# The low halves of the input projection's weights, split on VectorE instead of GpSimd

## The chip, the cores and the metric

The kernel runs on one core of a Trainium2 chip. The metric is the device time of one execution in microseconds (us). The engines are called PE (TensorE), DVE (VectorE), ACT (ScalarE), POOL (GpSimd) and SP (SyncE, which here issues most DMAs). Each works through its own instructions in the order in which the program lists them, and they wait for one another by semaphores.

## The reference

One layer of a decoder, for a prompt of 1024 tokens and 8 sequences of 4 new tokens each (1056 tokens in all), with a model width of 1024:

```python
h = rmsnorm(x, g_mix_norm)
q, k, v, b_gate, c_gate, hc = split(h @ w_in)       # 512 | 128 | 128 | 512 | 512 | 512
q, k = rope(rmsnorm(q, g_q)), rope(rmsnorm(k, g_k)) # 8 query heads, 2 key heads of 64
o_attn = window_attention(q, k, v, sinks)           # window of 128; new tokens use a cache
u = c_gate * hc
o_conv = b_gate * conv3(u)                          # depthwise, causal, width 3
x = x + concat(rmsnorm(o_attn), rmsnorm(o_conv)) @ w_o
x = x + square(relu(rmsnorm(x) @ w_up)) @ w_down    # 1024 -> 4096 -> 1024
x = x + sigmoid(rmsnorm(x) @ w_ple_gate) * (p @ w_ple)
```

All of it is float32.

## The kernel before

Activations are held with features in the partitions and the 1056 tokens in three chunks of 352 columns. Every large product is made from halves: a float32 matrix w is turned into w_hi, a copy rounded to the type that PE multiplies fast, and w_lo = w - w_hi, and the product is the sum of three: w_hi by x_hi, w_hi by x_lo, w_lo by x_hi.

The work is cut into units. A unit is one tile of 128 output features: 8 tiles of weights (128 x 1024 numbers in all), and for each chunk c of tokens 24 products of 128x128 by 128x352 into the PSUM bank acc[c] (`fill`, L1542, products at L1534). The input projection has 18 units: 0 to 5 make q, k and v, and 6 to 17 make the convolution's inputs in four groups of three (c_gate, hc, b_gate; `which` = 0, 1, 2). Then come 8 units of the output projection, 64 of the MLP and 8 of the gate.

The weights have two slots, used in turn. SP loads a unit's weights into w_st (L522) when the low half of the unit two before it, which used the same slot, has been made. ACT makes w_hi at the head of a unit for the next one, when PE is done with the unit before (`split_hi`, L799 to L805). Then the low half is made (`split_lo`, L498 to L501), and PE waits for it at the start of the next unit (L1700). In the input projection POOL makes the low halves (L757 to L758), but for the first two, which DVE makes while the tokens come in (L1170 to L1173); in all later stages DVE makes them.

Each engine runs one loop over g = 3 * unit + chunk. A list made ahead (`plan_inproj`, L67) puts the steps of attention on it, for 9 tiles of tokens t = 0 to 8, the first with the new tokens, starting at g = 18, 22, 25, 28 and so on. The steps of a tile, by their distance from its start, are: B (0, turn q, k, v to token rows), E (1, norm and rotary), S (3, turn back), Q (4, scores, maxima and exponentials), P and R (6 and 7, turn the probabilities, in two halves), V and W (7 and 8, the output's two halves), N and O (9, norm of the output, and turn it). So the head of each unit from 10 on has step W of one tile.

What the prediction speaks of, by line. On DVE: L1226 and L1228 (step E, low halves of q and k), L1235 (step S), L1281 (P and R, low halves of the probabilities), L1297 and L1305 (V and W, add and scale the output), L1347 (unit with `which` 1: u = c_gate * hc, from PSUM), L1365 (`which` 2: two taps of the convolution for each chunk) and L1372 (times b_gate). On ACT: L805 (high half), L888, L895 and L900 (step S), L935 (W, copies what L1297 adds), L943 (W, square of the output). On POOL: L501 (low half), L735 (W, after L943) and L747 (sum of squares of the convolution). On PE: L1549 (transposes), among them those of the probabilities. At the head of a unit DVE's order is: the convolution's instructions of chunk 0 (L1347, or L1365 twice and L1372, or none), then the steps of attention.

Of the kernel before, what the change touches and what calls it, by code (L numbers as in the profile page):

```python
# [139 lines left out]
def hybrid_step(nc, ins, outs):  # L140
# [149 lines left out]
    with ctx:  # L290
# [134 lines left out]
        def chunk(c):  # L425
            return slice(c * CH, (c + 1) * CH)
# [21 lines left out]
        def conv_parts(c):  # L448

            lo, hi = c * CH, min((c + 1) * CH, SEQ)  # L450
            parts = [(slice(0, hi - lo), (lo, hi))]
            if (c + 1) * CH > SEQ:
                parts.append((slice(SEQ - c * CH, CH), None))
            return parts
# [18 lines left out]
        def done_with(eng, *name):  # L473

            bank, _, before = aux_at[name]
            eng.wait_ge(aux_free[bank], before + 1)
# [21 lines left out]
        def split_lo(eng, s, his):  # L498

            eng.wait_ge(whi_ready, his)  # L500
            eng.tensor_tensor(w_lo[:, s, :], w_st[:, s, :], w_hi[:, s, :], ALU.subtract).then_inc(wlo_ready, 1)  # L501
# [141 lines left out]
        def _(pool):  # L643
# [97 lines left out]
            def add_squares(k):  # L741

                c = k % NCH
                pool.wait_ge(squared, k + 1)
                if k:
                    pool.wait_ge(summed, k)
                pool.tensor_tensor(sq_sum[:, chunk(c)], sq_sum[:, chunk(c)], sq_new[:, :], ALU.add).then_inc(summed, 1)  # L747

            def lo_of_attention(c):

                pool.wait_ge(att_hi, c + 1)
                pool.tensor_tensor(act_lo[:, 0:4, chunk(c)], qkv[:, 0:4, chunk(c)], act_hi[:, 0:4, chunk(c)],
                                   ALU.subtract).then_inc(att_lo, 1)

            for g in range(3 * U_OUT):
                u, c = divmod(g, NCH)
                if c == 0 and u >= 1:  # L757
                    split_lo(pool, (u + 1) % 2, u + 2)  # L758
                gated = u >= U_CONV and (u - U_CONV) % 3 == 2
                if gated and u == U_OUT - 1:  # L760
                    add_squares((u - U_CONV) // 3 * NCH + c)
                for step, t in at[g]:
                    consume(step, t)
                if gated and u < U_OUT - 1:
                    add_squares((u - U_CONV) // 3 * NCH + c)
                if u >= U_CONV and c == 0:
                    j, which = divmod(u - U_CONV, 3)
                    if which == 0:

                        done_with(pool, "C", 0, "c")  # L770
                        if j >= 1:
                            pool.wait_ge(conv_step, CONV_STEPS * j)
                            pool.wait_ge(tail_kept, 2 * j)
                        pool.tensor_copy(u_s[:, :, 0:2], state[:, j, :, :]).then_inc(u_state, 1)
                    if which == 2:

                        pool.wait_ge(acc_free[NCH - 1], u)
                        pool.tensor_copy(tail[:, j, 0:2], u_p[:, SEQ:SEQ + 2]).then_inc(tail_kept, 1)
                        pool.tensor_copy(tail[:, j, 2:2 + 2 * DEC_B].rearrange("p (b s) -> p b s", s=2),
                                         u_s[:, :, DEC_T:DEC_T + 2]).then_inc(tail_kept, 1)  # L780
                if g > 3 * U_OUT - NCH:
                    lo_of_attention(c - 1)
# [6 lines left out]
            for k in range(3 * KT):  # L789
                c = k % (2 * NCH) // 2  # L790
# [352 lines left out]
        def _(dve):  # L1143
# [169 lines left out]
            def norm_conv(c):  # L1313

                done_with(dve, "norm", c, 0)
                dve.reciprocal(root_c[:, c % 2, :], root_c[:, c % 2, :]).then_inc(conv_inverted, 1)
                dve.memset(sq_sum[:, chunk(c)], 0.0).then_inc(sums_cleared, 1)
                dve.wait_ge(conv_inverted, c + 1)
                for k in range(CT):
                    e = dve.scalar_tensor_tensor(out=conv[:, k, chunk(c)], in0=conv[:, k, chunk(c)],  # L1320
                                                 scalar=vec[:, V_CONV + k:V_CONV + k + 1], in1=root_c[:, c % 2, :],
                                                 op0=ALU.mult, op1=ALU.mult)
                e.then_inc(conv_normed, 1)

            def mix_conv(c):

                dve.wait_ge(mix_hi, c + 1)
                dve.tensor_tensor(act_lo[:, 4:8, chunk(c)], conv[:, :, chunk(c)], act_hi[:, 4:8, chunk(c)],
                                  ALU.subtract).then_inc(mix_lo, 1)

            for g in range(3 * U_OUT):
                u, c = divmod(g, NCH)
                if u >= U_CONV:
                    j, which = divmod(u - U_CONV, 3)
                    cw = [vec[:, V_CW + k * CT + j:V_CW + k * CT + j + 1] for k in range(3)]
                    if which == 1:

                        dve.wait_ge(acc_full, g + 1)
                        dve.wait_ge(acc_free[c], u)
                        for cols, tokens in conv_parts(c):  # L1340
                            if tokens is None:
                                dst = u_s[:, :, 2:2 + DEC_T]
                                e = dve.tensor_tensor(dst, acc[c][:, cols].rearrange("p (b s) -> p b s", s=DEC_T), dst,
                                                      ALU.mult)
                            else:
                                dst = u_p[:, 2 + tokens[0]:2 + tokens[1]]
                                e = dve.tensor_tensor(dst, acc[c][:, cols], dst, ALU.mult)  # L1347
                        e.then_inc(acc_free[c], 1)
                    if which == 2:

                        if c == 0:
                            dve.wait_ge(acc_free[NCH - 1], u)
                            dve.wait_ge(const_set, 7)
                            dve.wait_ge(u_state, j + 1)
                        done = CONV_STEPS * j + 2 + 2 * c
                        for cols, tokens in conv_parts(c):
                            for k in range(1, 3):
                                if tokens is None:
                                    dst = conv[:, j, SEQ:NT].rearrange("p (b s) -> p b s", s=DEC_T)
                                    src = u_s[:, :, k:k + DEC_T]  # L1360
                                else:
                                    dst = conv[:, j, tokens[0]:tokens[1]]
                                    src = u_p[:, tokens[0] + k:tokens[1] + k]
                                dve.wait_ge(conv_step, done)
                                dve.scalar_tensor_tensor(out=dst, in0=src, scalar=cw[k], in1=dst, op0=ALU.mult,  # L1365
                                                         op1=ALU.add).then_inc(conv_step, 1)
                                done += 1

                        dve.wait_ge(acc_full, g + 1)
                        dve.wait_ge(conv_step, done)  # L1370
                        dst = conv[:, j, chunk(c)]
                        dve.tensor_tensor(dst, acc[c][:, 0:CH], dst, ALU.mult).then_inc(acc_free[c], 1)  # L1372
                if g == 3 * U_OUT - 2:
                    norm_conv(0)
                if g == 3 * U_OUT - 1:
                    mix_conv(0)
                    norm_conv(1)
                for step, t in at[g]:
                    consume(step, t)
# [142 lines left out]
        def _(pe):  # L1522
            def take_bank(*name):

                bank, _, before = aux_at[name]
                if before:
                    pe.wait_ge(aux_free[bank], before)
                return aux[bank]
# [346 lines left out]
```

## Time and profile before

| | before |
|---|---|
| time, median of 3 runs | 1413.86 us |
| the runs | 1413.86, 1415.95, 1413.68 us |
| span of the profiled execution | 1409.7 us |
| PE, DVE, ACT, POOL busy in it | 1315.8, 716.3, 401.9, 199.2 us |

The profile is of one execution; its own time is given as its span, from the first to the last instruction. The runs' times have some 4 us around that. An engine's busy time is the sum in which it executed an instruction. A chain of waits follows the work back from the last instruction, at each step to what released it. In a timeline each line is an instruction, or several in a row merged; in brackets stands how long its engine had been idle and what released it. The granted clock of PE is given as a share of full speed.

### The profile page before, as it was taken

What the parts mean: (1) busy time and instruction counts of PE and PEld (TensorE: products, weight loads), DVE (VectorE), ACT (ScalarE), POOL (GpSimd) and SP (SyncE); (2) the same over time, 40 slices, a digit from 0 to 9 for tenths busy, and PEclk for the clock granted to TensorE, in tenths of its full rate; (3) what the DMA queues carried; (4) which work ended last, traced back from release to release, by engine and by line L of the source; (5) the groups of instructions that cost most, each with busy time, mean ns of one, the idle gap of its engine ahead of it and who ended that gap; (6) DMA issues with size and microseconds to landing.
All of it is one profiled execution on the core that took longest, in us unless ns stands there. A gap on an engine that the chain in (4) does not pass through costs nothing.

```text
span 1409.7 us, 21751 instructions
## 1 busy us (share of the span) xinstructions
PE 1315.8 (93%) x8348; PEld 1298.5 (92%) x8348; DVE 716.3 (51%) x1271; ACT 401.9 (29%) x801; POOL 199.2 (14%) x216
## 2 busy tenths in 40 slices
PE   3899988997958889999999999999999999999997
PEld 2899877897958889999999999999999999999997
DVE  6302757677575446435445344354453544587342
ACT  5332445455434222102111011121110211254232
POOL 6623434434130000000000000000000000041000
PEclk9999999999989899999999999999999999999999
DMA  5521011001103221321111111111111111111221
GB/s 153 131 60 32 1 48 30 16 16 35 46 17 75 62 65 41 77 52 45 48 47 54 45 45 45 45 45 45 45 45 45 45 50 39 46 45 54 69 68 46
DMA packets 111132, 70.99 MB, mean 50 GB/s; under 512 B 3226, under 2 KB 109622, under 8 KB 111064
## 3 DMA queue, kind: packets, MB, share of 16 engines
q1 hardware_dynamic: 110584, 68.37, 17.7%
q0 software_dynamic: 480, 1.93, 0.5%
q8 instruction: 33, 0.54, 0.2%
q14 instruction: 19, 0.16, 0.0%
q10 hardware_dynamic: 16, 0.00, 0.0%
HBM read 65.69 MB, written 5.54 MB: 51 GB/s over the span
## 4 chain that ended last, share of the span: by engine, by line
PE 77%; DVE 8%; ACT 4%; issue 4%; DMA 3%; POOL 2%; SPq 1%; DVEq 0%; ACTq 0%
PE acc L1534 71%; PE aux L1549 3%; DMA x_col<-in_x_sample 2%; DVE prob L1265 2%; PE aux L1534 1%; POOL act_lo L669 1%; DVE conv L1365 1%; POOL sq_sum L793 1%; DMA w_st<-in_w_in 1%; PE aux L1682 1%; DVE ropea L1218 1%; DVE o_tok L1305 1%; ACT sq_new L1097 1%; DVE pt_lo L1281 1%; ACT w_hi L805 0%
## 5 line engine op out<-in xcount | busy, mean ns | idle before, releaser
L1534 PE MATMUL acc<-xg_hi,w_hi 128*128 128x352 f32 x960 | 312.0, 325 | 0.0
L1534 PE MATMUL acc<-xg_lo,w_hi 128*128 128x352 f32 x960 | 307.8, 321 | 0.0
L1534 PE MATMUL acc<-xg_hi,w_lo 128*128 128x352 f32 x960 | 307.7, 321 | 0.0
L1534 PE MATMUL acc<-a_hi,w_hi 128*128 128x352 f32 x768 | 247.7, 323 | 0.0
L1534 PE MATMUL acc<-a_lo,w_hi 128*128 128x352 f32 x768 | 246.1, 320 | 0.0
L1534 PE MATMUL acc<-a_hi,w_lo 128*128 128x352 f32 x768 | 245.9, 320 | 0.0
L1534 PE MATMUL acc<-act_hi,w_hi 128*128 128x352 f32 x624 | 215.1, 345 | 13.2 <-issue 12.8
L1534 PE MATMUL acc<-act_hi,w_lo 128*128 128x352 f32 x624 | 208.3, 334 | 0.0
L1534 PE MATMUL acc<-act_lo,w_hi 128*128 128x352 f32 x624 | 208.2, 334 | 0.0
L1449 DVE TENSOR_TENSOR xt<-acc,xt 128x352 f32<-128x352 f32 x192 | 100.3, 522 | 179.1 <-PE acc L1534 178.1
L805 ACT ACTIVATE w_hi<-w_st 128x1024 fp32r<-128x1024 f32 x98 | 102.9, 1050 | 280.0 <-PE acc L1534 273.8
L1534 PEld LDWEIGHTS acc<-xg_lo,w_hi 128*128 128x128 f32 x960 | 180.5, 188 | 0.2
L1534 PEld LDWEIGHTS acc<-xg_hi,w_hi 128*128 128x128 f32 x960 | 180.1, 188 | 0.3 <-issue 0.2
L1534 PEld LDWEIGHTS acc<-xg_hi,w_lo 128*128 128x128 f32 x960 | 180.0, 188 | 0.0
L1534 PEld LDWEIGHTS acc<-a_lo,w_hi 128*128 128x128 f32 x768 | 144.3, 188 | 0.0
L1534 PEld LDWEIGHTS acc<-a_hi,w_hi 128*128 128x128 f32 x768 | 144.1, 188 | 0.0
L1534 PEld LDWEIGHTS acc<-a_hi,w_lo 128*128 128x128 f32 x768 | 143.9, 187 | 0.0
L793 POOL TENSOR_TENSOR sq_sum<-sq_sum,sq_new 128x352 f32<-128x352 f32 x24 | 23.2, 966 | 837.8 <-ACT sq_new L1097 837.8
L1534 PEld LDWEIGHTS acc<-act_hi,w_hi 128*128 128x128 f32 x624 | 124.8, 200 | 14.2 <-issue 13.2
L1068 ACT ACTIVATE a_hi<-relu 128x352 fp32r<-128x352 f32 x96 | 47.9, 499 | 292.6 <-DVE relu L1432 292.6
L1432 DVE SCALAR_TENSOR_TENSOR relu<-acc,rstd 128x352 f32<-128x352 f32 x96 | 50.3, 524 | 154.5 <-PE acc L1534 154.5
L1534 PEld LDWEIGHTS acc<-act_lo,w_hi 128*128 128x128 f32 x624 | 124.7, 200 | 0.0
(199 smaller groups left out, 1598.6 us busy)
## 6 DMA issues: line engine op xcount, KB each, us to landing
w_st<-in_w_up SPq DMA_DIRECT2D x32, 512.0 KB, 4.1
w_st<-in_w_down SPq DMA_DIRECT2D x32, 512.0 KB, 3.4
w_st<-in_w_in SPq DMA_DIRECT2D x18, 512.0 KB, 3.9
w_st<-in_w_o SPq DMA_DIRECT2D x8, 512.0 KB, 4.6
w_st<-in_w_ple_gate SPq DMA_DIRECT2D x8, 512.0 KB, 4.3
x_nat<-in_x_prompt SPq DMA_DIRECT2D x11, 352.0 KB
x_col<-in_x_prompt SPq DMA_DIRECT2D x8, 484.0 KB
out<-y_col SPq DMA_DIRECT2D x8, 484.0 KB
```

Of the source, the lines that this page charges most:

```text
L669: pool.tensor_tensor(act_lo[:, 4 * h:4 * h + 4, cols], h_tmp[:, h, :, :], act_hi[:, 4 * h:4 * h + 4, cols], ALU.subtract).then_inc(h_lo, 1)
L793: pool.tensor_tensor(sq_sum[:, chunk(c)], sq_sum[:, chunk(c)], sq_new[:, :], ALU.add)\
L805: act.activation(w_hi[:, s, :], w_st[:, s, :], ACT.Copy).then_inc(whi_ready, 1)
L1068: act.activation(a_hi[:, m, chunk(c)], relu[:, f % 2, :], ACT.Square).then_inc(a_hi_ready, 1)
L1097: act.activation(sq_new[:, :], xt[:, 2 * m + n2, chunk(c)], ACT.Square).then_inc(squared, 1)
L1218: dve.tensor_tensor(heads(ropea, m), qn, cos[:, None, :].broadcast_to([m, NQ + NKV, HD]), ALU.mult).then_inc(cos_ready, 1)
L1265: e = dve.tensor_tensor_reduce(prob[:, h * 2 * P:(h + 1) * 2 * P] .rearrange("p (s k) -> p s k", s=2), bank[:, cols].rearrange("p (s k) -> ...
L1281: frees(dve.tensor_tensor(pt_lo[0:rows_, cols], bank[0:rows_, 0:width], pt_hi[0:rows_, cols], ALU.subtract), step, t, i)
L1432: dve.scalar_tensor_tensor(out=relu[:, f % 2, :], in0=acc[c][:, 0:CH], scalar=0.0, in1=rstd[:, chunk(c)], op0=ALU.max, op1=ALU.mult)\
L1449: dve.tensor_tensor(xt[:, n, chunk(c)], acc[f % 3][:, 0:CH], xt[:, n, chunk(c)], ALU.add)\
L1534: ins_ = pe.matmul(out, w[a][cols], x[b][tile_], start=(k == 0 and p == 0), stop=(k == len(terms) - 1 and p == 2))
L1549: ins_ = pe.transpose(out[dst], src, ident[0:src.shape[0], 0:src.shape[0]])
```

## The change

`split_lo` for the units of the input projection is called on DVE at the head of each unit from 1 on, before everything else that DVE does there, and no longer on POOL. What it waits for (`whi_ready`), computes and signals (`wlo_ready`) is the same; the DVE loop and the POOL loop run over the same g.

```diff
--- before
+++ after
@@ POOL @@
             for g in range(3 * U_OUT):
                 u, c = divmod(g, NCH)
-                if c == 0 and u >= 1:
-                    split_lo(pool, (u + 1) % 2, u + 2)
                 gated = u >= U_CONV and (u - U_CONV) % 3 == 2
@@ DVE @@
             for g in range(3 * U_OUT):
                 u, c = divmod(g, NCH)
+                if c == 0 and u >= 1:
+                    split_lo(dve, (u + 1) % 2, u + 2)
                 if u >= U_CONV:
```

## Rows read from the trace of the kernel before

**Rows 1.** The page: span, busy time by engine, chain by engine.
```profile
span 1409.7 us, 21751 instructions
...
PE 1315.8 (93%) x8348; PEld 1298.5 (92%) x8348; DVE 716.3 (51%) x1271; ACT 401.9 (29%) x801; POOL 199.2 (14%) x216
...
PE 77%; DVE 8%; ACT 4%; issue 4%; DMA 3%; POOL 2%; SPq 1%; DVEq 0%; ACTq 0%
```
**Rows 2.** Busy time by stretch: its length, each engine, PE's granted clock, DMA share, GB/s.
```profile
41.20:131.00 89.80, 89.32 (x565) 88.38 (x564) 14.52 (x24) 29.04 (x57) 35.69 (x39) 1.00 0.25 68
131.00:404.00 273.00, 235.07 (x1576) 226.74 (x1574) 184.50 (x394) 132.01 (x346) 105.92 (x113) 0.94 0.10 27
...
270.90:274.30 3.40, 3.40 (x15) 3.40 (x13) 3.16 (x5) 1.36 (x4) 1.96 (x2) 0.50 0.02 5
218.40:222.50 4.10, 4.10 (x29) 4.06 (x28) 3.44 (x5) 1.31 (x4) 2.58 (x3) 1.00 0.00 0
```
**Rows 3.** Waits, 131 to 404 us: us in total, times, longest.
```profile
ACT aux L943 <- DVE o_tok L1305: 22.2, 8, 4.4
PE aux L1549 <- ACT qt L895: 21.6, 7, 6.3
```
**Rows 4.** Chain of waits, 228 to 246 us: start, us, what.
```profile
237.13 2.59 DVE conv L1365
```
**Rows 5.** Instructions of line 501: shortest, median and longest in ns.
```profile
L501 DVE TENSOR_TENSOR w_lo<-w_st,w_hi x81: 1216/1226/2836, 15.0 to 1372.0; 128x1024 fp32r<-128x1024 f32 x81
L501 POOL TENSOR_TENSOR w_lo<-w_st,w_hi x17: 2346/2398/2772, 63.4 to 380.8; 128x1024 fp32r<-128x1024 f32 x17
```
**Rows 6.** Timeline at the head of unit 14: start, us, instruction.
```profile
314.91 0.42 DVE L1228 TENSOR_TENSOR st_k<-ropea,st_k 128x256 fp32r<-128x256 f32 x1
...
315.24 3.19 DVE L1365 SCALAR_TENSOR_TENSOR conv<-u_p,vec,conv 128x352 f32<-128x352 f32 x2
315.30 2.76 POOL L501 TENSOR_TENSOR w_lo<-w_st,w_hi 128x1024 fp32r<-128x1024 f32 x1 [2.80 <-ACT w_hi L805]
...
318.54 0.53 DVE L1372 TENSOR_TENSOR conv<-acc,conv 128x352 f32<-128x352 f32 x1
...
319.43 0.43 DVE L1305 TENSOR_TENSOR o_tok<-o_tok,stats 128x256 f32<-128x256 f32 x1
319.77 0.58 DVE L1365 SCALAR_TENSOR_TENSOR conv<-u_p,vec,conv 128x352 f32<-128x352 f32 x1
319.89 0.60 ACT L943 ACTIVATE aux<-o_tok 128x512 f32<-128x512 f32 x1 [4.41 <-DVE o_tok L1305]
```
**Rows 7.** Timeline at the head of unit 13.
```profile
289.79 0.42 DVE L1228 TENSOR_TENSOR st_k<-ropea,st_k 128x256 fp32r<-128x256 f32 x1
...
290.12 0.52 DVE L1347 TENSOR_TENSOR u_p<-acc,u_p 128x352 f32<-128x352 f32 x1
290.17 2.38 POOL L501 TENSOR_TENSOR w_lo<-w_st,w_hi 128x1024 fp32r<-128x1024 f32 x1 [2.80 <-ACT w_hi L805]
...
291.00 1.83 DVE L1305 TENSOR_TENSOR o_tok<-o_tok,stats 128x256 f32<-128x256 f32 x1
...
292.87 0.60 ACT L943 ACTIVATE aux<-o_tok 128x512 f32<-128x512 f32 x1 [2.50 <-DVE o_tok L1305]
```
**Rows 8.** Timeline at the head of unit 12.
```profile
263.45 1.18 DVE L1228 TENSOR_TENSOR st_k<-ropea,st_k 128x256 fp32r<-128x256 f32 x1
...
264.87 0.42 DVE L1297 TENSOR_TENSOR o_tok<-aux,cross 128x256 f32<-128x256 f32 x1 [0.24 <-ACT cross L935]
265.33 1.82 DVE L1305 TENSOR_TENSOR o_tok<-o_tok,stats 128x256 f32<-128x256 f32 x1
...
267.18 0.60 ACT L943 ACTIVATE aux<-o_tok 128x512 f32<-128x512 f32 x1 [2.41 <-DVE o_tok L1305]
```
**Rows 9.** Chain of waits: two blocks of 24 products, units 10 and 12.
```profile
218.68 3.86 PE acc L1534 x24
...
271.43 5.21 PE acc L1534 x24
```

## The prediction, before the change was run

> **What bounds the kernel now.** I read the page first. TensorE (PE) is busy for 93% of the span and holds 77% of the chain that ended last; POOL, the engine that the work leaves, is busy for 14% and holds 2%, DVE, which gets it, 51% and 8% [rows 1]. On the page alone the change would be worth nothing, or would cost a little on the busier engine. So the second view was the table by stretches, to see whether the projection is one regime or two. It is two. From 41.2 to 131 us (units 0 to 6) PE is busy for 89.32 of 89.80 us and DVE for 14.52: there it does not matter who splits the weights. From 131 to 404 us (units 7 to 17, beside attention) PE is busy for 235.07 of 273.00 us, so 38 us of it are waits, although no engine is full: DVE 184.50, ACT 132.01, POOL 105.92 [rows 2]. Work passed from engine to engine one link at a time looks like this.
>
> The waits of that stretch name the link: ACT's square L943 waited 22.2 us in 8 waits for DVE's L1305, and PE's transposes L1549 waited 21.6 us in 7 waits for ACT's L895, which stands behind L943 in ACT's order [rows 3]. The chain of waits runs through the same place: a DVE instruction, L1365, with 2.59 us at 237.13 [rows 4]. In most other places it takes 0.58. To see why, one goes to the timeline at the head of a unit, where the moved instruction is.
>
> **Three kinds of head.** Unit u splits the weights of unit u+1 at its head: ACT the high half (L805), then POOL the low half (L501), 2.35 to 2.77 us there. The same instruction on DVE takes 1.22 in the middle, 2.84 at most [rows 5].
>
> In unit 14 POOL runs L501 from 315.30 to 318.06. DVE's pair of L1365 began at 315.24 and took 3.19 us, ending at 318.43, 0.37 after POOL was done; the next L1365 takes 0.58 with POOL idle. So the second of the pair stood still until POOL had finished: 3.19 less 2 x 0.58 and a gap of 0.04 is 1.99 us lost. L1372, L1297 and L1305 follow in DVE's order, and L943 starts 0.03 us after L1305 ends [rows 6]. Units 8, 11, 14 and 17 are of this kind, four heads.
>
> In unit 13 L1347 and L1297 stand there instead and are not stretched, but L1305 takes 1.83 us, against 0.43 in unit 14 with POOL idle, and ends 0.28 after POOL's split: 1.40 lost [rows 6, 7]. Units 10, 13 and 16 are of this kind.
>
> In unit 12 nothing of the convolution stands before L1297, and L1305 takes 1.82: 1.39 lost [rows 8]. Units 12 and 15 are of this kind.
>
> Unit 9 is neither: its tile's L1305 has run before the head, and DVE is idle there. I give it 0, as I do the first seven heads, which lie before or outside the serial stretch.
>
> **What the change removes, adds and moves.** It removes 17 instructions of about 2.4 us from POOL. Nobody waits for POOL's queue at the heads: L735, the next in it, waits for L943 anyway. What counts is that the stalls of DVE beside them go: 1.99, 1.40 and 1.39 us by kind.
>
> It adds 17 instructions on DVE. Their duration I take as the middle of the 81 that DVE has already, 1.22 us [rows 5]; the ends are 1.216 and 2.836. The long one needs POOL reading beside it, and POOL's only neighbour left at a head is the sum of squares L747, which in unit 12 already ends before DVE is free; hence the middle. On DVE consecutive instructions start about 0.08 us before the recorded end of the one before (289.79 plus 0.42 against 290.12 [rows 7]), so one more costs 1.22 - 0.04 to 0.08, some 1.18.
>
> It also adds a wait in DVE's queue: for the high half, by ACT. Queued behind it are L1365 or L1347, L1297 and L1305, and for them ACT and PE. This wait is nearly free: POOL's split starts at 315.30 released by ACT, when DVE's L1228 has just ended (315.33), and in unit 13 at 290.17 against 290.21 [rows 6, 7]. The reason is structural: ACT's high half directly follows the copies for which DVE's L1226 and L1228 wait. In unit 16, the last but one, there is no such copy any more; L1347, which there ran while DVE waited, goes behind the split, and I book that head like the others of its kind.
>
> By kind, with the split put in at the moment when DVE is free and the high half there:
> - units 8, 11, 14, 17: +1.18 - 1.99 = -0.8 each, -3.2 together. In unit 14: split 315.3 to 316.5, the pair to 317.6, L1372, L1297 and L1305 as long as now, L943 at 319.1 instead of 319.89.
> - units 10, 13, 16: +1.18 - 1.40 = -0.2 each, -0.6 together.
> - units 12, 15: L1228 ends at 264.63 and L1297 starts at 264.87, so 0.24 of the split lies in an idle gap, and the overlap hides some more: L1297 moves from 264.87 to 265.69, +0.82, and L1305 is shorter by 1.39: -0.57 each, -1.1 together.
>
> The sum is -4.9 us. What is late next: L943 has behind it on ACT L888, L895, L900 and the rest without a gap, and PE's waits for them, 21.6 us in 7, are 3.1 us each [rows 3], more than any gain. So PE does not become the bound and each gain is handed on whole, through the rest of the projection and to the end, since what follows starts from the end of this chain. In unit 17 the next product of PE may catch a part of the 0.8; a tenth or two. SP's queue gains: its load of the slot waits for the low half, which comes 1.5 us sooner in unit 14 (316.5 for 318.06), but no part of the chain above waits for a load.
>
> **The sum against a time.** The profiled execution has a span of 1409.7 us [rows 1]; the runs have a median of 1413.86, so 4.2 us lie around the span, and I take them as unchanged. 1409.7 - 4.9 = 1404.8 of span, 1408.9 of time, 0.35% less.
>
> **What else moves: TensorE's clock.** From 270.9 to 274.3 us the granted clock was 0.50, the 1.2 GHz level; from 218.4 to 222.5 it was 1.00, which is 2.4 GHz [rows 2]. The block of 24 products in the first took 5.21 us on the chain, in the second 3.86 [rows 9]. A wait that is shorter by 0.2 to 0.8 us can save such a stretch, and work that lies 5 us earlier can meet one elsewhere. One more or less is 1.4 us. I book nothing for it, and two either way in the range: 2.8 us.
>
> **Rivals.**
> *The trade is even.* The port time only changes its owner: 1.4 us of stall against 1.2 of split, as in unit 13, at all nine heads. Then it is 9 x 0.2 = 1.8 us, 1412.1. For it speaks unit 13; against it units 12 and 14, where the stall is longer or the split part hidden. The clock taking back three stretches (4.2 us) ends at the same place. Chance 0.15. The Trainium skill, page "Perfetto Trace Analysis", section "Optimizing Scalar/DVE Operations", warns of this: GpSimd and VectorE share a port to SBUF, so that moving work between the two might not help.
> *Shorter waits keep the clock up.* Three of the slow blocks become fast: 3 x 1.4 = 4.2 on top, 1404.7. For it: PE's waits at the heads, after which such a stretch stands in unit 12, all get shorter. Against: no row shows how short is short enough. Chance 0.13.
> *Slower: the stall stays.* DVE's stretched instructions wait for something else at the head than POOL's split (ACT's L805 reading the same tile, or another of POOL's that comes up into the free place). Then each of nine heads pays the split and gets nothing back: 7 x 1.18 + 2 x 0.82 = +9.9, 1423.8. It decides from about 0.55 us of stall left per head (4.9 over 9). Against it: at all three kinds the stretched instruction ends 0.3 to 0.4 us after POOL's, and the same forms are short at the same place without it. Chance 0.08. Splits of 2.84 us on DVE would end near there too (9 x 1.6 more).
> *It does not do what it says*: PE could wait for low halves that come later now. They come sooner (316.5 against 318.06), and they are needed a whole unit later. I give it nothing apart.
>
> **How the numbers follow.** Forecast 0.64, even trade 0.15, faster clock 0.13, stall stays 0.08. What a measurement of this kernel can tell from no change is 0.2%, 2.8 us, so faster is below 1411.0. Faster: 0.62 of the forecast's 0.64, 0.13, and 0.03 of the even trade, 0.78. Slower: 0.08. The same: 0.14. The forecast's own range is 1406.1 to 1411.7 (two slow blocks either way); with most of the faster clock and the even trade it is 1405.2 to 1412.6.
>
> **What would show it.** Right: L501 on DVE at 1.2 us, 17 more; at heads 8, 11, 14 and 17 L1365 at 0.58, at the others L1305 at 0.43; L943's wait for L1305 shorter; the stretch from 131 us to the first output unit shorter by 5 us and the MLP as long as before. Wrong: a stretched L1365 or L1305 at a head with POOL idle, a split of over 2 us, DVE idle at a head waiting for L805, or more stretches of granted clock 0.50 than now.

## The result, and the profile after

| | before | after |
|---|---|---|
| time, median of 5 runs | 1413.86 us (1412.80 to 1416.46) | 1404.06 us (1397.90 to 1407.85) |
| ratio after/before | | 0.9923, 95% interval 0.9898 to 0.9949 |
| span of the profiled execution | 1409.7 us | 1406.0 us |
| mean granted clock in it | 0.980 | 0.976 |

The kernel became faster, as forecast, but by 9.8 us and not by 4.9; 1404.06 lies 1.1 us under the range. The two profiled spans differ by only 3.7 us. Why the profiles show a smaller gain than the runs is the question of this part.

In the profile after, lines between L757 and L1331 carry numbers smaller by two (L941 is L943 of before, L1303 is L1305, L1226 is L1228). First the page: span, busy time, chain by engine, against [rows 1].

```profile
span 1406.0 us, 21751 instructions
...
PE 1317.5 (94%) x8348; PEld 1299.9 (92%) x8348; DVE 719.5 (51%) x1288; ACT 402.5 (29%) x801; POOL 158.3 (11%) x199
...
PE 80%; DVE 6%; ACT 4%; issue 3%; DMA 3%; POOL 3%; SPq 1%; DVEq 0%; ACTq 0%; POOLq 0%
```

DVE got 17 instructions and is busy for only 3.2 us more, although the splits take it 21 us, so its other instructions take some 18 us less. L1365 alone takes 8.1 us less in all (21.8 before, 13.7 after) and the scaling L1305 7.1 (13.9 and 6.8): the stall that has gone. POOL has 40.9 us less. Next the instructions of line 501, against [rows 5], and of the output's scaling on DVE (shortest, median and longest in ns).

```profile
L501 DVE TENSOR_TENSOR w_lo<-w_st,w_hi x98: 1207/1226/2831, 15.1 to 1368.3; 128x1024 fp32r<-128x1024 f32 x98
```
```profile
L1303 DVE TENSOR_TENSOR o_tok<-o_tok,stats x16: 424/426/427, 200.8 to 382.5; 128x256 f32<-128x256 f32 x16
```

No scaling is stretched any more (1.82 and 1.83 us in units 12 and 13 of before, 0.43 at most here). The head of unit 14, against [rows 6]: start, us, instruction.

```profile
310.45 0.42 DVE L1226 TENSOR_TENSOR st_k<-ropea,st_k 128x256 fp32r<-128x256 f32 x1
...
310.79 1.23 DVE L501 TENSOR_TENSOR w_lo<-w_st,w_hi 128x1024 fp32r<-128x1024 f32 x1
311.93 1.20 DVE L1365 SCALAR_TENSOR_TENSOR conv<-u_p,vec,conv 128x352 f32<-128x352 f32 x2
...
313.24 0.53 DVE L1372 TENSOR_TENSOR conv<-acc,conv 128x352 f32<-128x352 f32 x1
...
314.59 0.60 ACT L941 ACTIVATE aux<-o_tok 128x512 f32<-128x512 f32 x1 [3.56 <-DVE o_tok L1303]
```

From the end of L1226 (310.87) to the start of L941 it is 3.72 us; before, from 315.33 to 319.89, 4.56: -0.84. The split begins 0.08 us before L1226 has ended on the record, and the pair of L1365 takes 1.20. The heads of units 13 and 12, against [rows 7, 8]:

```profile
286.82 0.42 DVE L1226 TENSOR_TENSOR st_k<-ropea,st_k 128x256 fp32r<-128x256 f32 x1
...
287.17 1.23 DVE L501 TENSOR_TENSOR w_lo<-w_st,w_hi 128x1024 fp32r<-128x1024 f32 x1
288.31 0.52 DVE L1347 TENSOR_TENSOR u_p<-acc,u_p 128x352 f32<-128x352 f32 x1
...
289.19 0.43 DVE L1303 TENSOR_TENSOR o_tok<-o_tok,stats 128x256 f32<-128x256 f32 x1
...
289.66 0.60 ACT L941 ACTIVATE aux<-o_tok 128x512 f32<-128x512 f32 x1 [2.25 <-DVE o_tok L1303]
```
```profile
260.91 1.07 POOL L747 TENSOR_TENSOR sq_sum<-sq_sum,sq_new 128x352 f32<-128x352 f32 x1 [2.23 <-ACT sq_new L953]
261.08 1.18 DVE L1226 TENSOR_TENSOR st_k<-ropea,st_k 128x256 fp32r<-128x256 f32 x1
...
262.19 1.21 DVE L501 TENSOR_TENSOR w_lo<-w_st,w_hi 128x1024 fp32r<-128x1024 f32 x1
...
264.23 0.60 ACT L941 ACTIVATE aux<-o_tok 128x512 f32<-128x512 f32 x1 [1.82 <-DVE o_tok L1303]
```

Unit 13: 2.42 us from L1226 to L941, 2.66 before, -0.24. Unit 12: 1.97, 2.55 before, -0.58; there L1226 takes 1.18 us beside POOL's L747, as L1228 did before, and L747 has ended when the split starts. The waits over the serial stretch, against [rows 3]:

```profile
ACT aux L941 <- DVE o_tok L1303: 18.5, 8, 3.6
PE aux L1549 <- ACT qt L893: 17.9, 7, 6.4
```

Each is 3.7 us shorter. So at the three heads shown the mechanism is the one that was forecast. Now by stretches: units 7 to 17 and the output projection, before and after (length, PE, weight loads, DVE, ACT, POOL, granted clock, DMA, GB/s).

```profile
131.06:404.36 273.30, 235.01 (x1575) 226.71 (x1575) 184.80 (x395) 132.37 (x347) 105.86 (x113) 0.94 0.10 27
404.36:539.63 135.27, 114.58 (x676) 111.12 (x677) 70.50 (x119) 45.26 (x87) 7.57 (x4) 0.91 0.26 60
```
```profile
131.62:399.37 267.75, 235.19 (x1577) 226.63 (x1575) 178.73 (x406) 132.46 (x347) 78.46 (x102) 0.94 0.10 27
399.37:535.72 136.35, 116.26 (x676) 112.81 (x677) 71.13 (x119) 45.46 (x87) 7.55 (x4) 0.89 0.26 59
```

In units 7 to 17, 5.6 us are gone at the same clock. In the output projection, where the two kernels do the same work, 1.1 us came back at a clock of 0.89 instead of 0.91. The rest is 0.6 us lost before unit 7 and 0.2 after the output projection. So the two executions also differ in their clock where nothing was changed, and the runs have to be compared with their clocks beside them.

### The profile page after: what moved, and what is told of

Its sections match the earlier page's. It is cut to its first block, busy times and chain, and to the rows that moved or that the text cites. A ratio compares the mean times of both kernels' runs of the same rounds, so it can differ in the third digit from the quotient of the medians.

```text
span 1406.0 us, 21751 instructions
## 1 busy us (share of the span) xinstructions
PE 1317.5 (94%) x8348; PEld 1299.9 (92%) x8348; DVE 719.5 (51%) x1288; ACT 402.5 (29%) x801; POOL 158.3 (11%) x199
## 4 chain that ended last, share of the span: by engine, by line
PE 80%; DVE 6%; ACT 4%; issue 3%; DMA 3%; POOL 3%; SPq 1%; DVEq 0%; ACTq 0%; POOLq 0%
PE acc L1534 73%; PE aux L1549 3%; DMA x_col<-in_x_sample 2%; PE aux L1682 2%; PE aux L1534 1%; POOL act_lo L669 1%; DVE prob L1263 1%; POOL sq_sum L791 1%; ACT sq_new L1095 1%; DVE ropea L1216 1%; PE aux L1633 1%; ACT w_hi L803 0%; DVE pt_lo L1279 0%; DVE conv L1365 0%; SPq L580 0%
## 5 line engine op out<-in xcount | busy, mean ns | idle before, releaser
L501 DVE TENSOR_TENSOR w_lo<-w_st,w_hi 128x1024 fp32r<-128x1024 f32 x98 | 121.7, 1241 | 74.8 <-ACT w_hi L803 74.5
L1534 PEld LDWEIGHTS acc<-act_hi,w_hi 128*128 128x128 f32 x624 | 125.0, 200 | 13.9 <-issue 12.9
```

The costliest lines, as they stand in the source:

```text
L1534: ins_ = pe.matmul(out, w[a][cols], x[b][tile_], start=(k == 0 and p == 0), stop=(k == len(terms) - 1 and p == 2))
```

## The experiments

Theory 1: the stalls give about 5 us and PE's granted clock the rest. Theory 2: the stalls give about 10 in most executions. Theory 3: the heads that were given 0 give the rest. A run's mean granted clock (over its whole span) is listed beside its time, so the two terms can be told apart.

**The changed kernel again.**

> The changed kernel itself, timed again beside the kernel before, to see how far the gain repeats and what goes with it. Theory 1 (stalls and clock): the stalls of VectorE give the 5 us that the rows gave, and the rest of the 9.8 us is TensorE's granted clock, which is higher in most executions after the change because its waits at the heads are shorter. Then the mean granted clock of the changed kernel's runs lies some 0.003 to 0.005 above that of the runs before, and in either kernel a run that is longer has the lower clock (one stretch of 3.41 us at 1.2 GHz is 0.0012 of the mean clock and some 1.4 us). Ratio 0.992 to 0.996. Theory 2 (larger stalls): the heads give up 10 us in most executions and the profiled one was an exception; then the clocks of both kernels are alike and the times are not.

Median of 6 runs 1404.26 us, before 1413.51 (25 runs), ratio 0.9937 (0.9918 to 0.9957). All 11 runs of after have a mean clock of 0.9794, the 44 runs of before that were listed with it through this study 0.9764: the 0.003 of theory 1. Runs at the same clock can be set side by side:

| granted clock | before | after | difference |
|---|---|---|---|
| 0.976 | 1414.1 (17 runs) | 1407.5 (3 runs) | -6.6 |
| 0.981 | 1408.7 (5 runs) | 1403.0 (4 runs) | -5.7 |

Six of the 44 runs of before have a clock over 0.980. The profiled execution, with its 0.980, is near these.

Over all runs of all kernels of the study I fitted one slope for the clock and a level for each kernel: 1.10 us for 0.001 of mean clock, with a scatter of 1.1 us around it (one stretch of 3.41 us at half the clock is 0.0012 of the mean, by this 1.3 us). That all kernels share one slope is an assumption. "At equal clock" means the difference of two levels in this fit; against before its standard error is 0.3 to 0.5 us for the first four changed kernels and 0.6 to 0.8 for the others. All experiments in one table (us; times and clocks are means over the runs):

| kernel | runs | mean time | mean clock | against before, at equal clock | by the clock |
|---|---|---|---|---|---|
| before | 44 | 1413.5 | 0.9764 | | |
| after | 11 | 1404.3 | 0.9794 | -6.0 | -3.2 |
| heads of units 8, 11, 14, 17 | 12 | 1407.8 | 0.9782 | -3.7 | -2.0 |
| heads of units 10, 12, 13, 15, 16 | 6 | 1408.3 | 0.9790 | -2.4 | -2.8 |
| heads of units 1 to 7 and 9 | 12 | 1413.4 | 0.9767 | +0.1 | -0.3 |
| before, PE's waits filled | 8 | 1407.2 | 0.9848 | +2.8 | -9.2 |
| after, PE's waits filled | 4 | 1398.3 | 0.9872 | -3.4 | -11.9 |
| split after the steps | 5 | 1397.3 | 0.9814 | -10.7 | -5.5 |
| the same, waits filled | 5 | 1399.1 | 0.9828 | -7.4 | -7.0 |
| split after the steps from unit 10 on | 4 | 1395.4 | 0.9815 | -12.5 | -5.6 |

**The change in parts.** Each kernel takes a condition on u into both places:

```diff
-                if c == 0 and u >= 1:
+                if c == 0 and u >= 1 and not (u in (8, 11, 14, 17)):
                     split_lo(pool, (u + 1) % 2, u + 2)
...
+                if c == 0 and u >= 1 and (u in (8, 11, 14, 17)):
+                    split_lo(dve, (u + 1) % 2, u + 2)
```

> Only the heads of units 8, 11, 14 and 17 split on VectorE, all others on GpSimd as before. Theory 1: -3.2 us from the stalls (the second L1365 of each of these heads at 0.58 instead of 2.6 us), and a part of the clock's gain, since the longest waits of TensorE (units 11 and 14) are the ones that get shorter: -3 to -7 us in all. Theory 2: two thirds of the gain, -6.5 us, with the clock as before. Theory 3 (the early heads, or GpSimd left idle, gave the rest): -3.2 us and no more.

> Only the heads to which the prediction gave 0 split on VectorE: units 1 to 7 and 9. Theory 1: within 1.5 us of before, clock as before. Theory 3: -4 to -5 us.

> Only the heads of units 10, 12, 13, 15 and 16 split on VectorE, all others on GpSimd. The parts of the change run so far differ from the kernel before, at equal granted clock, by -6.0 us (all heads), -3.7 (units 8, 11, 14, 17) and 0.0 (units 1 to 7 and 9). Theory 1 (stalls by kind of head, the rest clock): -1.7 by the prediction's rows, -2.3 by what is left, at equal clock; as measured -1.5 to -4. Rival (the trade is even at these heads): 0, within 1 us.

Medians 1407.03, 1413.61 and 1409.08; ratios 0.9960 (0.9944 to 0.9976), 1.0003 (0.9985 to 1.0022) and 0.9951 (0.9934 to 0.9968). The early heads give nothing, so theory 3 falls. The parts at equal clock, -3.7, -2.4 and +0.1, add up to -6.0, the whole. By time alone the first part (-6.5 by the medians, -5.7 in the mean) would also suit theory 2, which wanted -6.5 with the clock as before; but the clock was 0.0018 higher, with a standard error of 0.0006. The trade is not even at the other heads either. The clock's terms of the parts, 2.0, 2.8 and 0.3, add up to 5.1 and not to the 3.2 of the whole; each is uncertain by some 1 us, so whether they add stays open.

**The clock alone.** The kernel before, with the stalls left in; PE repeats the last four products of step S in place while it would wait.

```diff
+                        again = {2: 12, 3: 2, 4: 7, 5: 4, 6: 2, 7: 7, 8: 4}.get(t, 0) if name == "k" else 0
-                        for f in range(4):
+                        for f in list(range(4)) * (1 + again):
```

> The kernel before, all splits on GpSimd, but TensorE repeats the last four products of step S (the turned keys, same result in the same place) 2 to 12 times over for tiles 2 to 8, in time in which it waited at the heads of units 9 to 15: 1 to 6 us of work more in each wait. The stalls of VectorE stay. Theory 1: the granted clock stays at 2.4 GHz in most of the stretches at 186 to 353 us, mean clock up by 0.003 to 0.008, time -3 to -9 us. Theory 2: no gain, 0 to +3 us, since nothing of the chain got shorter.

Median 1407.07, ratio 0.9956 (0.9936 to 0.9975). The stalls are all there, as the first line below shows for L1305 (longest 1.95 us) beside ACT's wait for it in the second, as long as before [rows 3], and yet the kernel is 6 us faster. So theory 2, which expected no gain here, falls: the clock alone can give as much as that.

```profile
L1305 DVE TENSOR_TENSOR o_tok<-o_tok,stats x16: 424/426/1945, 208.0 to 388.3; 128x256 f32<-128x256 f32 x16
...
  ACT aux L943: 22.2, 8
```

Its profile, of the slowest of its 8 runs, shows PE busy for 15 us more in units 7 to 17, at a clock of 0.96 instead of 0.94:

```profile
131.26:404.94 273.68, 250.23 (x1728) 240.96 (x1727) 185.79 (x395) 132.53 (x347) 106.05 (x113) 0.96 0.10 27
```

In this one execution the stretch is no shorter; over 8 runs the clock gave 9.2 us and the repeated products took 2.8. From 186 to 353 us, where the repeated products are, the clock stayed up as theory 1 expected: 0.98, against 0.93 before. In the profile of the changed kernel it is 0.91:

```profile
186.00:353.00 167.00, 144.03 (x967) 139.74 (x968) 116.01 (x257) 87.61 (x240) 71.77 (x77) 0.93 0.11 30
```
```profile
186.00:353.00 167.00, 157.61 (x1143) 152.16 (x1142) 116.11 (x256) 88.25 (x241) 71.91 (x77) 0.98 0.11 31
```
```profile
186.00:353.00 167.00, 149.64 (x997) 144.94 (x998) 112.84 (x264) 87.70 (x240) 52.99 (x68) 0.91 0.09 27
```

The first line is of before, the second of before with the waits filled, the third of after. Both profiles kept of the changed kernel are of runs at 0.976, the lowest clock among its 11, so no trace shows in which stretches its other runs kept the clock up; that it rises by 0.003 rests on the runs.

> The changed kernel with the same repeated products of step S as in the filled kernel before. Theory 1: stalls and clock are two terms that add, so that it differs from the filled kernel before (1407.2 us, mean clock 0.985) by the 6 us that the change gives at equal clock: 1400 to 1402 us, clock 0.984 to 0.986. Rival: the change's gain is the clock's in the main and TensorE's filled waits take it all: 1406 to 1408 us, as the filled kernel before.

Median 1397.82, ratio 0.9876 (0.9861 to 0.9890). Against the filled kernel before it is 8.9 us in the mean, 6.2 at equal clock: the same 6 us as without filling. So filling PE's waits takes nothing of the 6 us away, and the rival falls. The time is 2 us below what theory 1 expected; the clock, 0.9872, is above its range too, 0.002 over that of the filled kernel before.

**A later place for the split.** The split can cost the chain its 1.2 us at a head only where it stands ahead of the work that ACT waits for, and it is needed only a unit later.

```diff
-                if c == 0 and u >= 1:
-                    split_lo(dve, (u + 1) % 2, u + 2)
                 if u >= U_CONV:
...
                 for step, t in at[g]:
                     consume(step, t)
+                if c == 0 and u >= 1:
+                    split_lo(dve, (u + 1) % 2, u + 2)
```

> The split stays on VectorE, but at each head it comes after the head's steps of attention (behind L1297, L1305 and in units 8, 11, 14, 17 L1372) instead of ahead of them. VectorE then waits for ScalarE's and TensorE's next work for 1 us or more in most units, and the split lies there. Theory 1: the 1.18 us that the split costs the chain at each of nine heads goes: -8 to -10 us against the changed kernel at equal clock, 1393 to 1398 us. Rival: what comes next on VectorE (L1365 of the second chunk, L1235, the low halves of the probabilities) is as urgent, and the 1.2 us only move: 1402 to 1406 us.

Median 1396.43, ratio 0.9878 (0.9862 to 0.9894). The time is in the forecast window, but at equal clock it gained 4.7 us on the changed kernel where 8 to 10 were expected; the other 2.2 us of the difference in the mean are the clock's.

> Split on VectorE behind the head's steps of attention, and the repeated products of step S as well. Theory 1: both add up, 1390 to 1396 us at a clock of 0.984 or more. Rival: with the shorter waits the repeated products stand in TensorE's way (in the kernel before they cost 2.9 us at equal clock) and take back what the clock gives: as the kernel with the late split alone, or slower.

Median 1399.10, ratio 0.9888 (0.9870 to 0.9906): the rival. At equal clock the repeated products cost 3.3 us, and the clock gained 1.5.

> The split on VectorE ahead of everything at the heads of units 1 to 9, and behind the head's steps of attention from unit 10 on. The late split at all heads gave, at equal granted clock, 4.7 us against the changed kernel where 8 to 10 were expected, and its trace is 3 to 5 us late by unit 8, before any of the eight heads that it was meant for. If the early heads took that back (the split there stands behind steps that wait for ScalarE and GpSimd, and the next step waits for it): 3 to 5 us under the late split at all heads, 1391 to 1395 us. If the lateness at unit 8 was the clock's alone (two stretches at 1.2 GHz there): no difference at equal clock, 1395 to 1399 us.

Median 1395.42, ratio 0.9867 (0.9837 to 0.9898), at equal clock 1.8 us under the late split at all heads, with a standard error of 0.7 and 4 and 5 runs. That is between the two expectations: the early heads took back something, not 3 to 5. The traces agree: with the late split at all heads ACT's high half at unit 9 ends 4.6 us later than in the changed kernel (192.48 and 187.84 us), and here, with the early heads as in the changed kernel, still 3.0 later (190.84). The clock from 131 to 186 us is 0.94 in both, 1.00 in the changed kernel. So most of the lateness goes with the clock; of the 1.6 us between the two, 0.6 are there at unit 1 already, and 1.0 is left for the early heads.

Against the changed kernel it is 6.5 us less at equal clock. Over units 10 to 17 the time from the end of ACT's high half to L943 is 31.2 us in the profile before, 26.6 after and 18.7 here, 7.9 less than after: 0.8 to 1.2 at each head but that of unit 17, which gave 0.4. Where the 1.4 us between 7.9 and 6.5 went is not settled. Its head of unit 14, for DVE and then for ACT:

```profile
306.83 0.42 DVE L1226 TENSOR_TENSOR st_k<-ropea,st_k 128x256 fp32r<-128x256 f32 x1
307.17 1.20 DVE L1365 SCALAR_TENSOR_TENSOR conv<-u_p,vec,conv 128x352 f32<-128x352 f32 x2
...
309.36 0.42 DVE L1303 TENSOR_TENSOR o_tok<-o_tok,stats 128x256 f32<-128x256 f32 x1
309.70 1.22 DVE L501 TENSOR_TENSOR w_lo<-w_st,w_hi 128x1024 fp32r<-128x1024 f32 x1
310.83 1.20 DVE L1365 SCALAR_TENSOR_TENSOR conv<-u_p,vec,conv 128x352 f32<-128x352 f32 x2
```
```profile
309.81 0.60 ACT L941 ACTIVATE aux<-o_tok 128x512 f32<-128x512 f32 x1 [2.41 <-DVE o_tok L1303]
```

L941 starts 2.56 us after the end of L1226, against 3.72 in the changed kernel: the split's 1.2 us are gone from the chain. By the medians this is the fastest kernel of the study, 8.6 us under the changed one.

## Why the prediction was wrong

*What bounds the kernel: right.* The gain is in the serial stretch of units 7 to 17, and in none of the early heads (+0.1 us).

*Three kinds of head and their prices: right.* Measured in the traces from the end of ACT's high half to L943 (in unit 8, which has no L943, to L955 behind the convolution), the eight heads from 10 to 17 gave 4.6 us and unit 8 0.85, 5.5 together; 4.9 were forecast. By kind it is 0.84, 0.24 and 0.58 where 0.8, 0.2 and 0.57 stood; the stalls themselves, 14.9 us in all by the forecast's rows, are 15.2 in the totals of L1365 and L1305. The largest miss is unit 17, 0.98 for 0.8; this measure ends at L941 and does not show what PE caught behind it. At equal clock the runs give 6.0, with parts of 3.7 and 2.4 for 3.2 and 1.7; with a standard error of 0.4, that cannot be told from the 5.5.

*The added split and its wait: right.* 1.21 to 1.23 us at the heads, begun when L1226 ends, as the middle of the 81 said. *PE does not become the bound: right*, its waits for ACT are 17.9 us in 7 still.

*The clock: here it failed.* The step is "What else moves: TensorE's clock", where the prediction says "I book nothing for it, and two either way in the range". The clock was not neutral: it rose by 0.003 in the mean, worth 3.2 us, and in the means of the runs it rose wherever PE's waits got shorter (0.9782 and 0.9790 in the two halves of the change, 0.9767 where the splits moved but nothing of the chain did, 0.9848 where the waits were filled and nothing else). How much shorter a wait has to be is not shown. The rival "Shorter waits keep the clock up", with 1404.7 us and a chance of 0.13, is what happened, at 1404.06. That it came so close is in part luck: it added 4.9 and 4.2, and the runs show 6.0 and 3.2. The prediction had the row for it, a block of 24 products at 5.21 us beside one at 3.86 [rows 9], and counted it as chance of either sign, although it had named PE's waits at the heads as what such stretches follow and forecast that they shrink. *The trade is even* and *the stall stays* both fell with the parts and the trace after.

*One execution for all.* The trace of before had a clock of 0.980, when the mean of 44 runs is 0.9764. It came from the upper end, so that it showed fewer slow blocks than there are to win; the profile of after, at 0.976, is of the slowest of its 11 runs. That is why the two spans differ by only 3.7 us. By the fit it would be 1.6; two single executions with a scatter of 1.1 us each do not tell these apart. The 4.2 us that the prediction took to lie around the span were not that either: in every run of the study whose span is known the time is 1.8 us longer. The profiled execution was thus one of some 1411.5 us, quicker than all five runs of before.

## What to carry to other kernels

An engine's small share of busy time does not make its work free: look at what the neighbour's instructions last beside it and without it, and price a move by the stall that goes, less the time that comes. Where PE waits in a chain, its clock can be a second term with a sign: here every change that shortened its waits also raised the mean clock, so price it on that side. And before a profile is taken as typical, compare its mean granted clock with that of the runs.

## What was not expected of the hardware

The mean granted clock varies between executions of one program, from 0.973 to 0.983 in 44 runs of before, and with it the time, 1.1 us for 0.001, from 1417.8 to 1407.2. Work that computes nothing new can pay: the repeated products made the kernel before 6 us faster and the changed one too (1397.8 for 1404.1), but not the one with the late split (1399.1 for 1396.4). That its waits were already short fits, but was not tested.
